# The opening of a two-layer streaming encoder: first projection unit and input in quarters, vectors broadcast by DMA, late tables

## What is computed

```
for each layer l:
    xn = rmsnorm(x, g_mix)
    qa, ka, va, ga, ra, bb, cb, hb, qc, kc, vc = split_cols(xn @ w_in)      # 1024 x 3088
    y_a = gated linear attention(qa, ka, va, ga, ra)      # 4 heads, chunks of 64, carries a state
    y_b = short gated convolution(bb, cb, hb)             # 3 taps, carries 2 rows
    y_c = differential attention(rope(rmsnorm(qc)), rope(rmsnorm(kc)), vc)  # 4 heads x 2, with a cache
    x += concat(y_a, y_b, y_c) @ w_out
    x += ffn(rmsnorm(x, g_ffn))     # layer 0: SwiGLU, 2816 wide; layer 1: best 2 of 8 experts, 3584 wide
```

## Time and profile before

| | us |
|---|---|
| three runs | 1535.75, 1537.99, 1539.79 (median 1537.99) |
| the profiled execution | 1536.61, with a span of 1534.8 |
| busy in the span | TensorE 1525.0, VectorE 1233.9, ScalarE 998.2, GpSimd 218.5 |

### The profile page before, as it was taken

How to read it: one execution, slowest core, us unless ns; L and a number is a source line. 1 busy time by engine, 2 the same in 40 slices (tenths; PEclk the granted TensorE clock), 3 DMA queues, 4 the chain that set the end, 5 groups by cost and what they waited for, 6 DMA issues and landing times.

```text
span 1534.8 us, 21608 instructions
## 1 busy us (share of the span) xinstructions
PE 1525.0 (99%) x8428; PEld 1330.2 (87%) x8428; DVE 1233.9 (80%) x1254; ACT 998.2 (65%) x1078; POOL 218.5 (14%) x249
## 2 busy tenths in 40 slices
PE   9999999999999999999999999999999999999998
PEld 7999999999998988888888888888888888888887
DVE  5877666654577758988988888998998988898897
ACT  5565533333455547777777778777777777777775
POOL 5514400001150413101001001002002002002000
PEclk9999999999999999999999999999999999999999
DMA  8333445444433469999999999999999999999995
GB/s 226 96 110 128 144 157 165 145 144 151 132 115 110 142 217 366 381 371 386 371 377 380 377 369 377 388 364 383 381 372 377 380 366 373 396 365 367 396 367 185
DMA packets 159701, 437.43 MB, mean 285 GB/s; under 512 B 12068, under 2 KB 66176, under 8 KB 145264
## 3 DMA queue, kind: packets, MB, share of 16 engines
q1 hardware_dynamic: 151796, 423.02, 75.0%
q0 software_dynamic: 5552, 9.62, 2.3%
q10 hardware_dynamic: 2252, 3.41, 0.7%
HBM read 429.40 MB, written 13.60 MB: 289 GB/s over the span
## 4 chain that ended last, share of the span: by engine, by line
PE 98%; ACT 0%; DVE 0%; DMA 0%; issue 0%; SPq 0%; DVEq 0%; ACTq 0%
PE bank L1973 34%; PE bank L2468 13%; PE bank L2477 13%; PE bank L2472 13%; PE bank L2503 6%; PE bank L2506 6%; PE bank L2512 6%; PE bank L1976 3%; PE bank L2521 2%; PE bank L2495 0%; PE bank L2489 0%; PE bank L2488 0%; DMA gla<-b_g 0%; DVE x L1964 0%; ACT cut_hi L909 0%
## 5 line engine op out<-in xcount | busy, mean ns | idle before, releaser
L1801 DVE TENSOR_TENSOR split_lo<-raw,split_hi 128x2048 fp32r<-128x2048 f32 x336 | 762.7, 2288 | 101.8 <-ACT split_hi L1203 101.0
L1203 ACT CAST split_hi<-raw 128x2048 fp32r<-128x2048 f32 x336 | 640.5, 1911 | 224.7 <-PE bank L2477 145.8
L2468 PE MATMUL bank<-split_hi,xgT_hi 128*128 128x512 f32 x896 | 291.3, 395 | 0.0
L2472 PE MATMUL bank<-split_hi,xgT_lo 128*128 128x512 f32 x892 | 285.5, 390 | 0.0
L909 ACT CAST cut_hi<-ring 128x1024 fp32r<-128x1024 f32 x124 | 129.9, 1048 | 169.5 <-PE bank L1973 165.2
L2477 PE MATMUL bank<-split_lo,xgT_hi 128*128 128x512 f32 x896 | 239.7, 389 | 0.0
L1973 PE MATMUL bank<-xT_hi,cut_hi 128*128 128x320 f32 x752 | 235.4, 313 | 0.5 <-DVE cut_lo L1339 0.5
L1973 PE MATMUL bank<-xT_hi,cut_lo 128*128 128x320 f32 x752 | 232.3, 309 | 0.0
L1973 PE MATMUL bank<-xT_lo,cut_hi 128*128 128x320 f32 x752 | 230.7, 307 | 0.0
L1339 DVE TENSOR_TENSOR cut_lo<-ring,cut_hi 128x1024 fp32r<-128x1024 f32 x124 | 152.7, 1232 | 84.2 <-ACT cut_hi L909 83.4
L2477 PEld LDWEIGHTS bank<-split_lo,xgT_hi 128*128 128x128 f32 x896 | 168.2, 188 | 35.0
(11 more groups left out here) (311 smaller groups left out, 1721.2 us busy)
## 6 DMA issues: line engine op xcount, KB each, us to landing
raw<-moe_w_gate SPq DMA_DIRECT2D x112, 1024.0 KB, 8.0
raw<-moe_w_up SPq DMA_DIRECT2D x112, 1024.0 KB, 7.6
raw<-moe_w_down SPq DMA_DIRECT2D x112, 1024.0 KB, 7.4
ring<-w_in SPq DMA_DIRECT2D x15, 1024.0 KB, 5.5
ring<-ffn_w_gate SPq DMA_DIRECT2D x11, 1024.0 KB, 5.6
ring<-ffn_w_up SPq DMA_DIRECT2D x11, 1024.0 KB, 5.3
ring<-ffn_w_down SPq DMA_DIRECT2D x10, 1024.0 KB, 5.1
ring<-w_out SPq DMA_DIRECT2D x8, 1024.0 KB, 5.1
```

The source lines that it names most:

```text
L1203: return nc.scalar.copy(split_hi[:, i % SR, :], raw_piece(i)).then_inc(hi_ready, 1)
L1801: V.tensor_tensor(split_lo[:, i % SR, :], raw_piece(i), split_hi[:, i % SR, :].bitcast(F32), ALU.subtract).then_inc(lo_ready, 1)
L2468: TE.matmul(o, xgT_hi[:, kk, :], hi[:, w * k + 512 * c:w * k + 512 * c + 512], start=kk == 0, stop=False)
L2472: TE.matmul(o, xgT_lo[:, kk, :], hi[:, w * k + 512 * c:w * k + 512 * c + 512], start=False, stop=False)
```

## The change

- The first unit and the prompt's rows come in four quarters each (two feature blocks). ScalarE's queue has the identity and the prompt's quarters; SyncE's has g_mix, then the sample's rows (two halves) alternating with the first unit's quarters, and then the other parameters.
- TensorE runs 9 + 3 + 4 fillers. Only g_mix is transposed first; the rest of the parameters and the per-head gains are transposed together after the row transposes of kc 2. The transposes of x are spread among the matmuls of kc 0 and kc 1, which run quarter by quarter on two banks; the sample's tile is padded to 128 rows (cleared by VectorE). The unused bcast matmuls go: six transfers read each vector into all partitions.
- SyncE: the per-head gains in 2 transfers of whole rows instead of 24, the first layer's gate columns and the six broadcasts stand ahead of the fourth unit; constants in two parts, the later ahead of the fifth unit; the second layer's gate columns ahead of the seventh.
- The next two cuts (kc 2, qc 0) do the passes with the low weights last (`late_low`), so they can start when the high parts are there.
- GpSimd issues the loads of caches and states first, when the first unit has landed; the second layer's tables and the masks, router weights and gain factors come after the keys of the first layer are sent out.

```diff
-XT_RING = "CTCTSSOD"
+XT_RING = "TTSSODST"
...
-JOBS["T"] += [("bcast", 0), ("bcast", 1)]
-    JOBS["T"] += [("tok", "kc", _l, 0), ("tok", "kc", _l, 1)] + [("par2",)] * (_l == 0) + [("tok", "kc", _l, 2)]
+    JOBS["T"] += [("tok", "kc", _l, c) for c in range(3)] + [("par2",)] * (_l == 0)
...
+            for i in range(QUARTERS):
+                c = slice(QK * P * i, QK * P * i + QK * P)
+                if i < 2:
+                    sp.dma_start(xhat[0:DEC, 2, HALVES[i]], A["x_sample"][0][:, HALVES[i]]).then_inc(x_tail_in[i], 16)
+                sp.dma_start(ring[:, 0, 2 * QK * P * i:2 * QK * P * (i + 1)].rearrange("p (k n) -> p k n", k=QK),
+                             A["w_in"][0][c, KC:KC + 256].rearrange("(k p) n -> p k n", p=P)).then_inc(first_in[i] if i < QUARTERS - 1 else ring_full[0], 16)
...
             for n, u in enumerate(UNITS):
                 if n == 0:
-                    sp.wait_ge(x_in, 32)
+                    sp.wait_ge(x_in[QUARTERS - 1], 16)
                     continue
+                if n == 2:
+                    sp.dma_start(const[:, P:3 * P], A["const"][:, P:3 * P]).then_inc(ones_in, 16)
                 if n == RING:
                     head_gains()
+                    gate_columns(0)
+                    at = 0
+                    for name in ("g_q", "g_k", "lambda_q1", "lambda_k1", "lambda_q2", "lambda_k2"):
+                        w = DEPTH * A[name].shape[1]
+                        row = A[name].rearrange("l d -> (l d)").unsqueeze(0)
+                        sp.dma_start(bc[:, at:at + w], row.to_broadcast([P, w])).then_inc(bc_in, 16)
+                        at += w
+                if n == RING + 1:
+                    sp.dma_start(const[:, 3 * P:CONST_W], A["const"][:, 3 * P:CONST_W]).then_inc(const_in, 16)
+                if n == RING + 3:
+                    gate_columns(1)
...
+            pool.wait_ge(ring_full[0], 16)
+            loads(0)
             feature_rstd(0)
-            loads(0)
...
+            for i in range(QUARTERS):
+                for o in range(QK * i, QK * i + QK):
+                    x_hi(0, o)
+                act.wait_ge(first_in[i] if i < QUARTERS - 1 else ring_full[0], 16)
+                last = nc.scalar.copy(first_unit(cut_hi, i), first_unit(None, i))
...
+            V.memset(xhat[DEC:P, 2, :], 0.0).then_inc(x_pad, 1)
...
+            for i in range(QUARTERS):
+                for o in range(QK * i, QK * i + QK):
+                    x_lo(0, o)
+                first_lo(i)
+                if i == 0:
+                    residual(0, 0)
+                if i == 1:
+                    residual(0, 2)
...
                 if l == 0:
-                    residual(0, 3)
                     lo(q0 + 2)
-                    token_var()
...
                 to_rows(("kc", l, 1))
                 if l == 0:
-                    lambdas()
+                    token_var()
+                    residual(0, 1)
+                    residual(0, 7)
+                    lo(q0 + 3)
...
+            def late_low(R, job):
...
+                for k in range(KB):
+                    mm(b, w_hi[:, k], xT_hi[:, k, :], k == 0, False)
+                    mm(b, w_hi[:, k], xT_lo[:, k, :], False, False)
+                pe.wait_ge(cut_lo_ready, q + 1)
+                for k in range(KB):
+                    last = mm(b, w_lo[:, k], xT_hi[:, k, :], False, k == KB - 1)
+                last.then_inc(R.full, 1)
...
             pe.wait_ge(warm_zero, 1)
-            warm_up(20)
+            warm_up(9)
             pe.wait_ge(ident_in, 16)
-            pe.wait_ge(prow_in, 64)
-            tr(RT.begin(pe, ("par",))[:, 0:48], prow, 48).then_inc(RT.full, 1)
...
+            tr(RT.begin(pe, ("par",))[:, 0:16], prow[0:16], 16).then_inc(RT.full, 1)
+            warm_up(3)
+            pe.wait_ge(x_pad, 1)
...
+            for i in range(QUARTERS):
+                ks = range(QK * i, QK * i + QK)
+                if i == 0:
+                    pe.wait_ge(x_in[i], 16)
+                    pe.wait_ge(x_tail_in[0], 16)
+                    x_T(ks)
+                    warm_up(4)
+                elif i < QUARTERS - 1:
+                    next_x_T(i)
...
+                if i < QUARTERS - 1:
+                    high_high(ks)
+                    if i == 0:
+                        next_x_T(i)
+                    high_low(ks)
+                    pe.wait_ge(first_low, i + 1)
+                    low_high(ks)
...
+                    late_low(RC, ("kc", l, 2))
+                    rows_T("kc", 0)
+                    rows_T("kc", 1)
+                    late_low(RC, ("qc", l, 0))
+                    rows_T("kc", 2)
+                    pe.wait_ge(gains_in, 16 * 2)
+                    pe.wait_ge(prow_in, 48)
+                    b = RT.begin(pe, ("par2",))
+                    tr(b[:, 0:48], prow, 48)
+                    for k in range(3):
+                        last = tr(b[:, 64 + 4 * k:68 + 4 * k], prow2[:, P * k:P * k + P], 4)
+                    last.then_inc(RT.full, 1)
+                    pe.wait_ge(ones_in, 16)
```

More of the change, by code:

```diff
@@ L164 @@
 Q_FILL = 12
+QUARTERS = 4
 JOBS = {r: [] for r in "CTSOD"}
@@ L930, in _ @@
             act.wait_ge(RT.full, RT.filled(("par",)))
-            nc.scalar.copy(pcol[:, 0:48], RT.bank(("par",))[:, 0:48]).then_inc(RT.free, 1)
+            nc.scalar.copy(pcol[:, 0:16], RT.bank(("par",))[:, 0:16]).then_inc(RT.free, 1)
             act.wait_ge(RT.free, RT.emptied(("par",)))
@@ L951, in _ @@
             hi(3)
-            act.wait_ge(RT.free, RT.emptied(("xt", 3)))
-            for i in range(2):
-                act.wait_ge(RT.full, RT.filled(("bcast", i)))
-                nc.scalar.copy(bc[:, 288 * i:288 * i + 288], RT.bank(("bcast", i))[:, 0:288]).then_inc(RT.free, 1)
+            act.wait_ge(RT.free, RT.emptied(("xt", 7)))
             def lambdas():
@@ L2040, in warm_up, with x_T @@
             def warm_up(count):
                 for _ in range(count):
-                    mm(RD.bank(("xt", KB - 1))[:], warm[:, 0:P], warm[:], True, True)
+                    mm(RO.banks[0][:], warm[:, 0:P], warm[:], True, True)
+            def x_T(ks):
+                for k in ks:
+                    R, job = norm_end(0, k)
+                    b = R.begin(pe, job)
+                    for t in range(NT):
+                        last = tr(b[:, P * t:P * t + P], xhat[:, t, P * k:P * k + P], P)
+                    last.then_inc(R.full, 1)
@@ new lines, in _, with high_high, high_low @@
+            first = [(RC.begin(pe, ("kc", 0, j))[:, 0:T], split_cut(cut_hi, j), split_cut(cut_lo, j)) for j in range(2)]
+            def high_high(ks, which=first):
+                for k in ks:
+                    pe.wait_ge(xhi_ready, k + 1)
+                    for b, w_hi, w_lo in which:
+                        mm(b, w_hi[:, k], xT_hi[:, k, :], k == 0, False)
+            def high_low(ks, which=first):
+                for k in ks:
+                    pe.wait_ge(xlo_ready, k + 1)
+                    for b, w_hi, w_lo in which:
+                        mm(b, w_hi[:, k], xT_lo[:, k, :], False, False)
@@ L2045, in _, with low_high @@
+            def low_high(ks, which=first):
+                for b, w_hi, w_lo in which:
+                    for k in ks:
+                        last = mm(b, w_lo[:, k], xT_hi[:, k, :], False, k == KB - 1)
+                    if ks[-1] == KB - 1:
+                        last.then_inc(RC.full, 1)
             pe.wait_ge(warm_zero, 1)
-            warm_up(20)
+            warm_up(9)
             pe.wait_ge(ident_in, 16)
-            pe.wait_ge(prow_in, 64)
-            tr(RT.begin(pe, ("par",))[:, 0:48], prow, 48).then_inc(RT.full, 1)
@@ L2050, in _ @@
-            pe.wait_ge(x_in, 32)
-            for k in range(KB):
-                R, job = norm_end(0, k)
-                b = R.begin(pe, job)
-                for t, (t0, rows) in enumerate(TILES):
-                    last = tr(b[:, t0:t0 + rows], xhat[0:rows, t, P * k:P * k + P], rows)
-                last.then_inc(R.full, 1)
+            pe.wait_ge(mix_gain_in, 16)
+            pe.wait_ge(prow_zero, 1)
+            tr(RT.begin(pe, ("par",))[:, 0:16], prow[0:16], 16).then_inc(RT.full, 1)
```

181 lines of the change are left out of this document (98 added, 83 removed).

## The result

The changed kernel takes 1540.33 us (median of 10 runs, 1538.56 to 1542.69), the kernel before 1537.09 in the same session (10 runs, 1535.75 to 1539.79): ratio 1.0018 [1.0010, 1.0026]. The forecast was 1535.2 with a range up to 1538.6. The change is a loss of about 3 us (1.5 to 4.0 by the interval), inside the 0.3% but on the wrong side of nothing, and beyond the range.

A forecast was written before the change was run, and what follows sets the result against it. TensorE was taken as the bound, busy 1525.0 of 1534.8 us, so only the first 32 us could give. An earlier start gave 2.5 us and the rest 0.3, making 1533.8 profiled, 1535.2 as median, range 1531.6 to 1538.6.

The forecast's parts named there:

- the sum: Whole kernel: 2.8 us earlier at qc 1 and kept to the end, so 1533.8 us for the profiled execution.
- S: TensorE's opening: start of x's first transpose, taken as 6.65 us, bounded by 5.5 and 7.4, against 9.14 before.
- S + 2.7: TensorE's opening: first matmul of the two cuts, after two transposed blocks, one high part and one cast on ScalarE.
- Rival C: Opening: everything meets early, S = 5.5 and transposes no dearer; gain 4.9 us, 1533.1 us; chance 0.16.
- cost 0 to 0.5: Fourth unit on SyncE's queue: landing between 24.1 and 27.1 costs TensorE 0 to 0.5 us, upper bound 4.8, taken as 0.
- rival B: SyncE's queue: small pieces make the fourth unit late, landing at 38.8, and the kernel slower, 1546.4 us; chance 0.07.
- rival A: TensorE's opening: the clock rises later, costing up to 3.4 us; at 2, gain 0.8, 1537.2 us; chance 0.17.
- All of this is 0: GpSimd's moved loads, tables and constants, VectorE's new constants wait, lambdas, second-layer gate columns: all covered, costing nothing.
- (2): Experiments' theory, near 66 us: VectorE late for xhat because lambdas' second half and GpSimd's tables meet; wait 2.47 us.
- (1): Experiments' theory, before qc 1: broadcasts ahead make the fourth unit land late; the 2.70 us wait lets the clock fall.
- D: Opening: shared DMA engines land x's first quarter as late as the whole, S = 7.4; gain 0.6, 1537.4 us; chance 0.10.

The follow-up runs named there:

- e8: Changed kernel with GpSimd's second-layer tables and constants later, lambdas' second half at its old place, broadcasts behind the fifth unit: 1533.43 us, ratio 0.9967 to the kernel before.
- e5: Changed kernel with the first layer's gate columns ahead of the third unit, broadcasts and remaining constants behind the fifth: 1537.15 us, ratio 0.9998 to the kernel before.
- e3: Changed kernel with twelve filler matmuls ahead of the parameter transposes, in the wait of 2.70 us: 1540.03 us, ratio 1.0011 to the kernel before.
- e1: Changed kernel with GpSimd's second-layer tables and constants moved later, behind qb_ready: 1535.92 us, ratio 0.9990 to the kernel before.
- e4: Changed kernel with the lambdas' second half back at its old place on VectorE: 1535.74 us, ratio 0.9988 to the kernel before.
- e7: Kernel before the change, with only GpSimd's second-layer tables and constants moved behind the keys: 1538.32 us, ratio 0.9997 to the kernel before.
- e9: The changed kernel run again as it is: 1540.80 us, ratio 1.0024 to the kernel before.
- e11: Changed kernel with GpSimd's tables and constants later and the lambdas' second half at its old place, SyncE's order untouched: 1538.46 us, ratio 1.0003 to the kernel before.
- r11: Repeat of e11 (GpSimd's tables later, lambdas' second half at its old place) on one chip beside r8: 1537.15 us, ratio 1.0003 to the kernel before.
- r8: Repeat of e8 (tables later, lambdas back, broadcasts behind the fifth unit) on one chip beside r11: 1533.90 us, ratio 0.9978 to the kernel before.
- e6: Changed kernel with the six broadcasts replaced by same-shaped transfers from different rows of the cache; numbers differ, only the opening is read: 1536.71 us, one run.
- e2: Changed kernel with the first layer's gate columns and the six broadcasts behind the fourth unit: 1541.95 us, ratio 1.0027 to the kernel before.
- e10: Changed kernel with GpSimd's cache and state loads back behind the rstd of the features: 1542.01 us, ratio 1.0033 to the kernel before.

## Why the prediction was wrong

**The start was right, but the pieces of the sum were not.** S was put at 6.65 with 5.5 as the low end; it is 5.78. A pair of x blocks takes 0.66 us (six transposes at 10.26 and at 16.08 in the chain of e8), so 0.33 a block and not 0.68: six blocks were priced 2.1 us too dear. The padding was put at 0.9 us of cost, and the rows say the opposite. The unpadded block of 0.57 had its weight loads in front of the sample's 64 rows standing for 0.17 each time:

```profile
9.51 0.40 PEld L1976 LDWEIGHTS bank<-const_sb,xhat 64*128 64x128 f32 x3 [0.17 <-issue]
```

The padded blocks show no such gap. No run pads and changes nothing else, so that the padding is the cause is read from the rows, not shown. The first matmul at S + 2.7 = 9.3 was right as a number (9.43) for another reason: ScalarE stands 1.41 us for the first quarter of the unit, a transfer that I had covered. In all, qc 1 can start at 27.65 (e5), 4.8 us before the old one and not 2.8. Rival C's 4.9 was the better sum for the opening.

**The step that failed first is the fourth unit's "cost 0 to 0.5".** Its issue at 20.21 lies in my bounds. It took 7.53 to land, over the 5.1 to 7.3 taken, and TensorE needed it earlier than I said: it stood from 27.02 on, and with the 2.0 us from landing to release it needed the unit at 25.0, not at 26.6. Part of that is my own doing, the opening being 2 us faster than summed; cover was worked out against a schedule that the change itself moves forward. I priced each broadcast by its issue, 0.44, and gave it no time on the wire. Six of them took 6.1 us to issue, and there was a hole in the traffic behind them. The sign named for rival B, ScalarE standing before the cast of qc 2 beyond 27, is the one that showed: landing at 27.7, not the 38.8 that B was priced at. B had the kernel slower than before only from a landing at 30.4 on; it is slower with one at 27.7.

**A term was missing: the clock after a wait.** I looked for the clock only at the opening (rival A), where it held in the changed kernel's profile. It fell after the wait of 2.70, and made qc 1 5.23 instead of 3.50: 1.7 us. That it read 1.00 with e3's fillers speaks for the wait as its cause. Of the nine profiles with the changed kernel's order of transfers, the two with waits of 0.8 and 0.9 before qc 1 show 1.00 after them (e1, e4), and the six with waits of 1.4 to 2.9 without fillers all show the lower level. The waits for xhat are less regular, as the last section says.

**The second failed step is "All of this is 0", said of GpSimd's work.** I took 20.32 us in which GpSimd stood as free. It is free for GpSimd, but VectorE is busy in it, and GpSimd's work there holds up VectorE's: 2.50 for a copy of 0.80. The lambdas' second half was priced at 0 as well and takes 1.2 us of an engine without a gap. Either alone is hidden by what VectorE had to spare (e1, e4, e7); together they are not, and cost 2.47 of wait, with a fall of the clock in some executions (e5: 4.2 us in all). The Trainium skill, "GPSIMD Engine Reference", section "Key points", says that GpSimd shares its memory interfaces with VectorE and that they contend with VectorE instructions that have two operands in SBUF or run in a two-port mode. The trace agrees for the sum of two operands (1.21 for 0.55); for the copy, which has one, no row shows in which mode it ran.

**In numbers.** The profiled execution took 5.5 us more than the sum. At qc 2 the changed kernel stands at 36.52 where the sum had 34.2: 2.3, which is 0.6 at the start of qc 1 (30.22 against 29.6; the rest of the 2.70 is paid by the better opening) and 1.7 of clock. At the cut behind the wait for xhat it stands at 69.41 where the sum had 64.4: 5.0, so 2.7 more, of which 2.47 is that wait. The last 0.5 comes after 600 us and is not located.

**What the two waits cost.** With (2) taken away the ratio goes from 1.0024 to 1.0003 (e9 to e11, one chip); with (1) as well to 0.9978 (r11 to r8, one chip). So (2) is worth about 0.2% and (1) about 0.25%, and the rest, the earlier opening, is a gain of about 0.2 to 0.3%.

**Rules that I cited.** The Trainium skill, "DMA: Bandwidth & Descriptors", section "Specifications", with its least size of 512 bytes for the full rate, leaned to rival B, and to the right side: under the broadcasts the traffic fell to between 44 and 60 GB/s. But with pieces of the same size from different rows e6 has no such hole, so size is not all of it. The rule against the change, in the section "Rules for kernel authors" of that page of the Trainium skill, would have made it D, and D did not come: x's first transpose starts at 5.78, not at 7.4.

## What to carry to other kernels

A gain at the opening is kept only if everything that the faster engine needs next is early by as much: work out each transfer's cover against the new schedule, not the old. What is put ahead of a unit on a queue is priced by when the unit lands, and a broadcast in small pieces can cost microseconds; put it behind the last unit that is wanted soon, as in the version that beat both kernels (e8). An idle engine is no free place for work if, as here, its work lengthens that of a busy one.

## What the runs showed of the hardware

The kernel before has three levels of time, and they go with the granted clock over the run: of 113 runs in these sessions 13 had a mean clock of 0.996 (mean 1539.9 us), 48 of 0.997 (1538.1) and 52 of 0.998 and more (1536.1). The profiled execution that I read (1536.61) is of the last level, with a wait of 0.87 for the gate bias; e7's profile, the same opening with a wait of 2.10 there and 1.2 GHz after it, took 1540.19, as the first. So in these two profiles about 1 us in the landing of one small transfer goes with some 4 us of time; that it is what separates the levels in the other runs is not shown. The median of three runs, against which the forecast was set, can fall on any of the levels.

The clock does not fall at the wait: in the changed kernel TensorE resumed at 29.72, ran at the full pitch up to 31.4, and at the lower level to 34.9. Nor does it follow each such wait: the wait of 2.1 for the first quarter was followed by a fall in e8 and by none in r8, which is the same program. The waits for xhat of 2.62 (e5) and 2.71 (e9) were followed by a fall, those of 2.47 (the changed kernel), 2.62 (e2), 2.87 (e3), 2.88 (e6) and 2.10 (e10) by none. What decides between them is open.

Between VectorE and GpSimd either can be the one held: in the changed kernel a copy of VectorE's took 2.50 and GpSimd's products 0.5 to 0.7 (0.33 to 0.50 alone), in e7 VectorE's copy took 0.91 and GpSimd's products up to 1.75 (in e4 as well).
